# One kernel, two attentions: a query block moved ahead of the first scores, and three output tiles interleaved

## The chip, the cores and the metric

The kernel runs on one core of a Trainium2 chip. A core has TensorE (PE, matrix products), VectorE (DVE), ScalarE (ACT), GpSimd (POOL) and SyncE (SP, which here only issues DMAs). Each engine takes its own instructions in order, and they meet at semaphores. The metric is the device time of one launch in microseconds (us); the smaller, the better.

## The reference

The input is one sequence of 512 tokens of width 1024. Two blocks follow one another:

```
h1 = layer_norm(a*x  + stick_breaking(x) @ mix_wo)          # first attention, over the tokens
h2 = layer_norm(a*h1 + mem_cross_attn(h1, mem) )            # second attention, over 256 memory rows
h3 = layer_norm(a*h2 + (gelu(g) * val) @ ffn_down)          # g, val: h2 @ ffn_up through a short convolution
y  = h3 + rms_norm((gated sum of three branches of rms_norm(h3)) @ w_out)

def mem_cross_attn(h, mem, w_q, w_kv, w_o):                 # 4 heads of 256 columns
    q = heads(h @ w_q);  k, v = heads(split(mem @ w_kv))
    p = softmax(q @ k.T * 256 ** -0.5)
    return merge(p @ v) @ w_o
```

The change is in the second attention, `mem_cross_attn`, and in one helper that three other projections share.

## The kernel before, in words

Activations lie transposed, 128 features on the partitions and 512 tokens along the row, so a tensor of width 1024 is eight tiles of 128x512. float32 products are made out of three faster ones: each operand is cast to a high part (`_hi`, made by ACT) and a remainder (`_lo`, the value minus the high part), and a product is `w_lo*x_hi + w_hi*x_lo + w_hi*x_hi`. One "block" in this text is the three matmuls of one weight block of 128x128 (k counts the eight blocks of a tile), so an output tile is 24 matmuls of 128x512.

**Weights.** They come in units of 128x1024, one unit for one output tile. A ring of four slots holds them. SP loads unit u as soon as PE has counted unit u-4 into `unit_done`; ACT makes `w_hi` in two halves (`split_hi`, line 1551), POOL makes `w_lo` in two halves behind it (line 2261). Each half counts one in `whi_made` or `wlo_made`. ACT and POOL make the units in the order of the program, between their other work. `xq` are the eight query units, `xo` the eight units of the output projection; xo+3 below is the fourth of them. In the stretch of `xo` SP also loads four units of the feed-forward (`extra_stage`, line 535), each right behind a load of the ring (line 533).

**`two_products`** (lines 607 to 636) makes several tiles together in an order of (tile, block) pairs. It issues two matmuls of each block at once and the third, with the remainder of the activation (line 619), four blocks later (`LAG`). It waits for the whole of a unit's `w_lo` before the first block of that tile. **`product`** (lines 584 to 605) makes one tile; it waits for the first half of `w_lo` at block 0, for the second at block 4. `between` and `ahead` put other work into the order.

**Second attention on PE** (lines 863 to 914). Query tiles 0 and 1 are made by `two_products` while the normalization before still delivers `x_hi`, then `xa_scores(0)`. For each of the heads 1 to 3: two query tiles, `xa_turn` of the head before (eight transposes of its probabilities), `xa_scores` of this head (24 matmuls of 128x256 into banks 2 and 3), `xa_values` of the head before (12 matmuls into banks 6 and 7). ACT takes a query tile out of PSUM (line 1556), DVE makes its remainder (line 2684). The softmax of a head goes DVE maximum (2651, 2655), ACT exponential (1690), DVE division (2659). ACT and DVE make `o_hi` and `o_lo` of each half head (1703, 2672).

**Output projection** (lines 936 to 946). `two_products` makes tiles 0 and 1, in the order k = 0..7 with both tiles at each k; before its 11th block it turns head 3, before its 13th it makes head 3's values, whose `o_lo` (counted by `xa_o`) blocks k = 6 and 7 need. Tiles 2 to 5 follow one by one, then tiles 6 and 7 in halves of 256 tokens. A tile's result is taken by DVE: `xo_y` (2710) makes Y = a*H + tile, then `xo_add` and `xo_add_square` add it and its square into running sums; ACT squares it (`xo_square`, 1723).

**ACT's order from head 3 on** matters here:

```
xa_soft(3); split_hi(xo + 2); xa_take(3)
for n in range(7):
    xo_square(n)                 # waits for y of tile n
    if n < 5: split_hi(xo + n + 3)
```

POOL follows with `w_lo` of xo+3 to xo+7 (line 2283), each half when ACT has counted its high part.

Of the kernel before, what the change touches and what calls it, by code (L numbers as in the profile page):

```python
# [6 lines left out]
F32 = mybir.dt.float32  # L7
# [9 lines left out]
KB = D // P  # L17
HD_A = 64
PAIRS = D // P
XA_HEADS = 4  # L20
D_FF = 2816
FFB = D_FF // P
NS = SEQ // P
# [15 lines left out]
U0, _u = {}, 0  # L39
# [6 lines left out]
RING = 4  # L46
# [69 lines left out]
def build_block(nc, w, xT, memT, vec, const, small, pool_count, outT):  # L116
    ctx = ExitStack()
    with ctx:
# [162 lines left out]
        def OUT_BANK(t):  # L281
            return (U0["out"] + (0, 1, 0, 0, 1, 0, 0, 1)[t]) % 2 if t not in (2, 5) else 2
# [25 lines left out]
        JOINT_BANK = [(2, 2, 3, 3, 0, 0), (5, 5, 6, 6, 7, 7)]  # L308
        DOWN_BANK = [4, 1]
        WO_ACC, WO_ACC2 = 7, 5  # L310
        WO_BANKS = [1, 0, 3, 6, 4, 0, 1, 3]
        WO_READ = {5: 2, 6: 1, 7: 3}
        XO_BANK = [{6: 0, 7: 1}, {6: 2, 7: 3}]
# [38 lines left out]
        EV0 = {}  # L352
# [228 lines left out]
        def _(pe):  # L581
            pe.sem_inc(unit_done, CREDIT)

            def product(out, u, slot, hi, lo, ready=None, blocks=8, k0=0, last_k=None, done=True, between=None):


                pe.wait_ge(wlo_made, 2 * u + 1)
                for k in range(blocks):
                    if k == 4:
                        pe.wait_ge(wlo_made, 2 * u + 2)  # L590
                    if between is not None and k in between:
                        between[k]()
                    if ready is not None:
                        pe.wait_ge(*ready(k))
                    if slot is None:
                        wh, wl = unit_hi(u)[:, k * P:(k + 1) * P], unit_lo(u)[:, k * P:(k + 1) * P]
                    else:
                        wh, wl = w_hi[:, slot, k * P:(k + 1) * P], w_lo[:, slot, k * P:(k + 1) * P]
                    first = k0 + k == 0
                    end = k0 + k == (blocks - 1 if last_k is None else last_k)  # L600
                    pe.matmul(out, wl, hi(k), start=first, stop=False)  # L601
                    pe.matmul(out, wh, lo(k), start=False, stop=False)  # L602
                    mm = pe.matmul(out, wh, hi(k), start=False, stop=end)  # L603
                if done:
                    mm.then_inc(unit_done, 1)

            def two_products(u, hi, lo, hi_ready, lo_ready, order=None, ahead=None, banks=None):

                banks = banks or [(u + n) % 2 for n in range(2)]
                order = order or [(n, k) for k in range(4) for n in range(2)] + [(0, 4), (0, 5), (1, 4), (0, 6), (0, 7), (1, 5), (1, 6), (1, 7)]  # L610
                first_n = {n: order.index((n, k)) for n, k in reversed(order)}
                first_k = {k: order.index((n, k)) for n, k in reversed(order)}

                def low(at_n):
                    n, k = order[at_n]
                    b, slot = banks[n], (u + n) % RING
                    if first_k[k] == at_n:
                        pe.wait_ge(*lo_ready(k))
                    mm = pe.matmul(ps[:, b, :], w_hi[:, slot, k * P:(k + 1) * P], lo(k), start=False, stop=(k == KB - 1))
                    if k == KB - 1:  # L620
                        mm.then_inc(unit_done, 1)

                for at_n, (n, k) in enumerate(order):
                    b, slot = banks[n], (u + n) % RING
                    if ahead is not None and at_n in ahead:
                        ahead[at_n]()
                    if first_n[n] == at_n:
                        pe.wait_ge(wlo_made, 2 * (u + n) + 2)
                    if first_k[k] == at_n:
                        pe.wait_ge(*hi_ready(k))  # L630
                    pe.matmul(ps[:, b, :], w_lo[:, slot, k * P:(k + 1) * P], hi(k), start=(k == 0), stop=False)
                    pe.matmul(ps[:, b, :], w_hi[:, slot, k * P:(k + 1) * P], hi(k), start=False, stop=False)
                    if at_n >= LAG:
                        low(at_n - LAG)
                for at_n in range(len(order) - LAG, len(order)):
                    low(at_n)
# [197 lines left out]
            def tile(n, t, hi, lo, between=None):  # L834
                u = U0[n] + t
                if n == "out":
                    if t > 2:
                        pe.wait_ge(evac, t - 2 + (EV0[n] + CREDIT))
                elif n == "wo":
                    if t in WO_READ:  # L840
                        pe.wait_ge(y_made, WO_READ[t] + BEFORE["y_made"]["wo"] + CREDIT)
                elif t != 2:
                    pe.wait_ge(y_made, t + (BEFORE["y_made"][n] + CREDIT - 1))
                bank = OUT_BANK(t) if n == "out" else WO_BANKS[t] if n == "wo" else 6 if t == 2 else u % 2
                product(ps[:, bank, :], u, u % RING, hi, lo, between=between)

            def o_rows(k):
# [54 lines left out]
            for h in range(XA_HEADS):  # L902
                if h == 0:
                    two_products(U0["xq"], x_rows, x_rows_lo, lambda k: (xhi_made, k + 1 + BEFORE["xhi_made"]["wo"]),
                             lambda k: (x_ready, k + 1 + BEFORE["x_ready"]["wo"]))
                for d in range(2 if h else 0):
                    u = U0["xq"] + 2 * h + d
                    pe.wait_ge(evac, EV0["xq"] + 2 * h + d + CREDIT - 1)
                    product(ps[:, u % 2, :], u, u % RING, x_rows, x_rows_lo)
                if h:  # L910
                    xa_turn(h - 1)
                xa_scores(h)
                if h:
                    xa_values(h - 1)
            def xo_sums(half, parts=range(2)):
# [6 lines left out]
            def xo_half(t, half, between):  # L922

                u, o = U0["xo"] + t, ps[:, XO_BANK[half][t], HALF[half]]
                for k in range(KB):
                    if not half and k % 4 == 0:
                        pe.wait_ge(wlo_made, 2 * u + 1 + k // 4)
                    if k in between:
# [6 lines left out]

            pe.wait_ge(evac, EV0["xo"] + CREDIT)
            two_products(U0["xo"], o_rows, o_rows_lo, lambda k: (xa_o, k + 1), lambda k: (xa_o, k + 1),
                         [(n, k) for k in range(KB) for n in range(2)],
                         {10: lambda: xa_turn(XA_HEADS - 1), 12: lambda: xa_values(XA_HEADS - 1)})
            for t in range(2, KB - 2):  # L940
                tile("xo", t, o_rows, o_rows_lo)
            for t in (6, 7):
                pe.wait_ge(y_made, t - 1 + (BEFORE["y_made"]["xo"] + CREDIT))
# [594 lines left out]
        def _(act):  # L1538
# [166 lines left out]
            for h in range(XA_HEADS):  # L1705
                for d in range(2):
                    u = U0["xq"] + 2 * h + d
                    if h:
                        split_hi(u + 2)
                    take(xq_hi[:, 2 * h + d, :], u % 2, u + CREDIT + 1)  # L1710
                if h == 0:
                    split_hi(U0["xq"] + AHEAD)
                if h:
                    xa_take(h - 1)
                xa_soft(h)
            split_hi(U0["xo"] + 2)
            xa_take(XA_HEADS - 1)

            def xo_square(n):
# [766 lines left out]
        def _(dve):  # L2486
# [188 lines left out]
            def xa_parts(h):  # L2675

                two = slice(2 * h, 2 * h + 2)
                if h == 0:
                    dve.wait_ge(evac, EV0["xq"] + CREDIT)
                link(dve.tensor_copy(mk_hi[:, two, :], mem_k[:, two, :]))  # L2680
                dve.tensor_tensor(mk_lo[:, two, :], mem_k[:, two, :], mk_hi[:, two, :].bitcast(F32), ALU.subtract).then_inc(xa_split, 1)
                for d in range(2):
                    dve.wait_ge(evac, EV0["xq"] + CREDIT + 2 * h + d + 1)
                    dve.tensor_tensor(xq_lo[:, 2 * h + d, :], ps[:, d, :], xq_hi[:, 2 * h + d, :].bitcast(F32),
                                      ALU.subtract).then_inc(xa_split, 1)
                two = slice(2 * h * P, (2 * h + 2) * P)
                link(dve.tensor_copy(mv_hi[:, :, two], mem_v[:, :, two]))
                dve.tensor_tensor(mv_lo[:, :, two], mem_v[:, :, two], mv_hi[:, :, two].bitcast(F32), ALU.subtract).then_inc(xa_split, 1)
# [8 lines left out]
            def xo_y(n):  # L2697

                k, half = XO_PARTS[n]
                cols = xo_cols(n)  # L2700
                if half is None:
                    dve.wait_ge(unit_done, U0["xo"] + k + 1 + CREDIT)
                    bank = 6 if k == 2 else k % 2
                else:
                    if half:
                        dve.wait_ge(unit_done, U0["xo"] + k + 1 + CREDIT)
                    else:
                        dve.wait_ge(half_tile_s, k - 5)
                    bank = XO_BANK[half][k]
                dve.scalar_tensor_tensor(out=Y[:, k, cols], in0=H[:, k, cols], scalar=ALPHA, in1=ps[:, bank, cols],  # L2710
                                         op0=ALU.mult, op1=ALU.add).then_inc(y_made, 1)
# [611 lines left out]
```

## Time and profile before

| | |
|---|---|
| median of 3 runs | 1368.56 us (1368.35 to 1369.66) |
| profiled execution | 1367.44 us, its span 1365.7 us |
| PE busy | 1348.8 us, 99% of the span |
| POOL / DVE / ACT busy | 792.0 / 742.4 / 671.5 us |
| granted TensorE clock | full in all 40 slices |

The span is what the profiler sees between the first and the last instruction; 1.74 us of the execution lie outside it. Matmuls are pipelined: a row gives 0.39 us for one of 128x512, but in a stream one starts every 0.227 us. PE's real cost is therefore read from the starts, not from the durations. "Idle before" stands in brackets at the end of a timeline row, with the instruction that ended it.

### The profile page before, as it was taken

The page shows a single profiled execution, that of the slowest core. Times are in us where ns is not written, and L with a number is a line of the kernel's source. Part 1 is how long each engine was busy: PE and PEld are TensorE (multiplying, and loading weights), DVE is VectorE, ACT ScalarE, POOL GpSimd, SP SyncE. Part 2 cuts the span into 40 slices and gives each one's busy share as a digit, 9 for nine tenths or more (in the row PEclk, how much of TensorE's full clock was granted, in tenths as well). Part 3 has the DMA queues.
Part 4 walks back from the last instruction along what each step waited for, and adds up shares of the span by engine and source line. Part 5 has one row for each costly group of instructions (what it writes and reads, how often), then busy time and mean ns, then how long its engine had stood idle before and what let it go on. Part 6 is the DMA issues. An engine that isn't in the chain of part 4 may idle for free.

```text
span 1365.7 us, 24197 instructions
## 1 busy us (share of the span) xinstructions
PE 1348.8 (99%) x9438; PEld 1139.1 (83%) x9438; DVE 742.4 (54%) x995; ACT 671.5 (49%) x1176; POOL 792.0 (58%) x599
## 2 busy tenths in 40 slices
PE   9999999999999999999999999999999999999998
PEld 7888787778899888888888887788888878999987
DVE  5135466465555333333544957344279857777732
ACT  4245665463456444443322578566473435445543
POOL 7653343463466566655665647854268856666782
PEclk9999999999999999999999999999999999999999
DMA  6332221321230232233323212200023222323322
GB/s 228 127 121 77 78 78 47 119 82 62 90 127 32 96 105 92 92 100 100 105 96 109 106 62 93 78 4 4 18 78 124 93 93 93 107 98 106 100 101 77
DMA packets 34508, 122.81 MB, mean 90 GB/s; under 512 B 3824, under 2 KB 4336, under 8 KB 34288
## 3 DMA queue, kind: packets, MB, share of 16 engines
q1 hardware_dynamic: 33696, 119.31, 26.0%
q10 hardware_dynamic: 720, 2.20, 0.5%
q8 instruction: 67, 1.10, 0.3%
q14 instruction: 25, 0.20, 0.0%
HBM read 119.40 MB, written 2.10 MB: 89 GB/s over the span
## 4 chain that ended last, share of the span: by engine, by line
PE 90%; DVE 4%; POOL 2%; ACT 2%; issue 1%; DMA 0%; SPq 0%; ACTq 0%; DVEq 0%; POOLq 0%
PE ps L601 16%; PE ps L602 16%; PE ps L603 16%; PE ps L1452 3%; PE ps L1454 3%; PE ps L1453 3%; PE ps L1521 1%; PE ps L1520 1%; PE ps L1522 1%; PE ps L728 1%; PE ps L753 1%; PE ps L741 1%; PE ps L957 1%; POOL w_lo L2261 1%; PE ps L972 1%; PE ps L973 1%
## 5 line engine op out<-in xcount | busy, mean ns | idle before, releaser
L2261 POOL TENSOR_TENSOR w_lo<-stage,w_hi 128x512 fp32r<-128x512 f32 x378 | 554.1, 1491 | 361.8 <-ACT w_hi L1551 356.9
L1551 ACT ACTIVATE w_hi<-stage 128x512 fp32r<-128x512 f32 x376 | 215.4, 623 | 112.2 <-DMA stage<-w 97.1
L601 PE MATMUL ps<-x_hi,w_lo 128*128 128x512 f32 x664 | 262.6, 395 | 0.0
L602 PE MATMUL ps<-x_lo,w_hi 128*128 128x512 f32 x664 | 258.6, 389 | 0.0
L603 PE MATMUL ps<-x_hi,w_hi 128*128 128x512 f32 x664 | 258.6, 389 | 0.0
L601 PEld LDWEIGHTS ps<-x_hi,w_lo 128*128 128x128 f32 x664 | 124.6, 188 | 29.3 <-issue 2.6
L603 PEld LDWEIGHTS ps<-x_hi,w_hi 128*128 128x128 f32 x664 | 124.6, 188 | 26.3
L602 PEld LDWEIGHTS ps<-x_lo,w_hi 128*128 128x128 f32 x664 | 124.7, 188 | 25.7 <-issue 1.0
L2445 POOL TENSOR_TENSOR w_lo<-stage,w_hi 128x512 fp32r<-128x512 f32 x44 | 75.3, 1743 | 54.0 <-DVE s_val L3165 54.0
L2799 DVE SCALAR_TENSOR_TENSOR conv<-ps,vcol,conv 128x511 f32<-128x511 f32 x44 | 33.0, 749 | 132.2 <-ACT conv L1771 132.0
L1771 ACT ACTIVATE conv<-ps,vcol 128x512 f32<-128x512 f32 x44 | 34.3, 779 | 121.1 <-PE ps L603 120.1
L2549 DVE TENSOR_TENSOR_SCAN ps<-ps,self_one 128x512 f32<-128x512 f32 (+1 forms) x64 | 49.2, 815 | 26.2 <-ACT ps L1613 26.2
L601 PE MATMUL ps<-f_hi,w_lo 128*128 128x512 f32 x154 | 59.9, 389 | 0.0
L602 PE MATMUL ps<-f_lo,w_hi 128*128 128x512 f32 x154 | 59.9, 389 | 0.0
L603 PE MATMUL ps<-f_hi,w_hi 128*128 128x512 f32 x154 | 59.9, 389 | 0.0
L2301 POOL TENSOR_TENSOR f_lo<-conv,f_hi 128x512 f32 (+1 forms) x22 | 28.5, 1297 | 43.6 <-ACT f_hi L1783 43.6
L3174 DVE TENSOR_TENSOR s_lo<-s_val,s_hi 128x512 fp32r<-128x512 f32 x33 | 51.1, 1601 | 0.0
L1383 PE MATMUL ps<-x_hi,w_lo 128*128 128x512 f32 x128 | 50.4, 394 | 0.4 <-POOL w_lo L2261 0.4
L2376 POOL TENSOR_TENSOR Mk<-blk,levels 128x256 f32<-128x256 f32 x40 | 28.5, 731 | 37.5 <-PE ps L1319 16.8
L1385 PE MATMUL ps<-x_hi,w_hi 128*128 128x512 f32 x128 | 49.9, 389 | 0.0
L1384 PE MATMUL ps<-x_lo,w_hi 128*128 128x512 f32 x128 | 49.8, 389 | 0.0
L1520 PE MATMUL ps<-ys_hi,w_lo 128*128 (+1 forms) x96 | 37.5, 390 | 0.0
(516 smaller groups left out, 3316.6 us busy)
## 6 DMA issues: line engine op xcount, KB each, us to landing
stage<-w SPq DMA_DIRECT2D x210, 512.0 KB, 3.3
extra_stage<-w SPq DMA_DIRECT2D x6, 512.0 KB, 5.0
H<-xT SPq DMA_DIRECT2D x3, 512.0 KB, 8.2
mem<-memT SPq DMA_DIRECT2D x2, 512.0 KB, 10.9
pool_n<-pool_count ACTq DMA_DIRECT2D x1, 1024.0 KB, 6.5
outT<-outs SPq DMA_DIRECT2D x4, 256.0 KB, 2.0
outT<-outs SPq DMA_DIRECT2D x2, 384.0 KB, 2.7
stage<-w SPq DMA_DIRECT2D x2, 256.0 KB, 3.5
```

Of the source, the lines that this page charges most:

```text
L601: pe.matmul(out, wl, hi(k), start=first, stop=False)
L602: pe.matmul(out, wh, lo(k), start=False, stop=False)
L603: mm = pe.matmul(out, wh, hi(k), start=False, stop=end)
L1383: pe.matmul(o, wl, x_hi[:, k, :], start=(k == 0), stop=False)
L1384: pe.matmul(o, wh, x_lo[:, k, :], start=False, stop=False)
L1385: mm = pe.matmul(o, wh, x_hi[:, k, :], start=False, stop=(k == KB - 1))
L1520: pe.matmul(o, wl, hi, start=(k == 0), stop=False)
L1551: act.activation(unit_hi(b)[:, cols], unit_stage(b)[:, cols], ACT.Copy).then_inc(whi_made, 1)
L2261: pool.tensor_tensor(unit_lo(b)[:, cols], unit_stage(b)[:, cols], unit_hi(b)[:, cols].bitcast(F32), ALU.subtract).then_inc(wlo_made, 1)
L2445: pool.tensor_tensor(w_lo[:, slot, cols], stage[:, slot, cols], w_hi[:, slot, cols].bitcast(F32), ALU.subtract).then_inc(wlo_made, 1)
L2549: dve.tensor_tensor_scan(z, z, self_one[:, SEQ - n:SEQ][:, ::-1], 0.0, ALU.mult, ALU.add).then_inc(link_s, 1)
L3174: dve.tensor_tensor(s_lo[at_n][:], s_val[at_n][:], s_hi[at_n][:].bitcast(F32), ALU.subtract).then_inc(st_lo_s, 1)
```

## The change

Five edits, all in the second attention but for the first:

1. In `two_products`, a tile's first block waits for the first half of its `w_lo` alone, and block 4 waits for the second half.
2. Query tile 2 goes to bank 6 in place of bank 0 and no longer waits for tile 0's evacuation. Its block k = 0 is issued ahead of `xa_scores(0)`, its other seven behind.
3. `two_products` of the output projection makes tiles 0, 1 and 2 together (banks 0, 1, 2): 24 blocks in place of 16. Ten blocks (k = 0..4 of tiles 0 and 1) come first; then block (2,0), head 3's turn, (0,5), (1,5), head 3's values, (2,1) to (2,5), and k = 6 and 7 of all three tiles. Ahead of (2,0) PE waits for the exponentials of head 3, which read bank 2.
4. The single tiles begin with tile 3.
5. ACT makes `w_hi` of xo+2 before `xa_soft(3)` in place of behind it.

```diff
--- before.py
+++ after.py
@@ -308,6 +308,8 @@
         JOINT_BANK = [(2, 2, 3, 3, 0, 0), (5, 5, 6, 6, 7, 7)]
         DOWN_BANK = [4, 1]
         WO_ACC, WO_ACC2 = 7, 5
+        XQ_BANKS = [0, 1, 6, 1, 0, 1, 0, 1]
+        XO_BANKS = [0, 1, 2, 1, 0, 1]
         WO_BANKS = [1, 0, 3, 6, 4, 0, 1, 3]
         WO_READ = {5: 2, 6: 1, 7: 3}
         XO_BANK = [{6: 0, 7: 1}, {6: 2, 7: 3}]
@@ -625,6 +627,8 @@
                     if ahead is not None and at_n in ahead:
                         ahead[at_n]()
                     if first_n[n] == at_n:
+                        pe.wait_ge(wlo_made, 2 * (u + n) + 1)
+                    if k == KB // 2:
                         pe.wait_ge(wlo_made, 2 * (u + n) + 2)
                     if first_k[k] == at_n:
                         pe.wait_ge(*hi_ready(k))
@@ -839,9 +843,9 @@
                 elif n == "wo":
                     if t in WO_READ:
                         pe.wait_ge(y_made, WO_READ[t] + BEFORE["y_made"]["wo"] + CREDIT)
-                elif t != 2:
+                else:
                     pe.wait_ge(y_made, t + (BEFORE["y_made"][n] + CREDIT - 1))
-                bank = OUT_BANK(t) if n == "out" else WO_BANKS[t] if n == "wo" else 6 if t == 2 else u % 2
+                bank = OUT_BANK(t) if n == "out" else (WO_BANKS if n == "wo" else XO_BANKS)[t]
                 product(ps[:, bank, :], u, u % RING, hi, lo, between=between)
 
             def o_rows(k):
@@ -904,12 +908,14 @@
                     two_products(U0["xq"], x_rows, x_rows_lo, lambda k: (xhi_made, k + 1 + BEFORE["xhi_made"]["wo"]),
                              lambda k: (x_ready, k + 1 + BEFORE["x_ready"]["wo"]))
                 for d in range(2 if h else 0):
-                    u = U0["xq"] + 2 * h + d
-                    pe.wait_ge(evac, EV0["xq"] + 2 * h + d + CREDIT - 1)
-                    product(ps[:, u % 2, :], u, u % RING, x_rows, x_rows_lo)
+                    n, u = 2 * h + d, U0["xq"] + 2 * h + d
+                    if n > 2:
+                        pe.wait_ge(evac, EV0["xq"] + n + CREDIT - 1)
+                    product(ps[:, XQ_BANKS[n], :], u, u % RING, x_rows, x_rows_lo,
+                            between={1: lambda: xa_scores(0)} if n == 2 else None)
                 if h:
                     xa_turn(h - 1)
-                xa_scores(h)
+                    xa_scores(h)
                 if h:
                     xa_values(h - 1)
             def xo_sums(half, parts=range(2)):
@@ -935,9 +941,11 @@
 
             pe.wait_ge(evac, EV0["xo"] + CREDIT)
             two_products(U0["xo"], o_rows, o_rows_lo, lambda k: (xa_o, k + 1), lambda k: (xa_o, k + 1),
-                         [(n, k) for k in range(KB) for n in range(2)],
-                         {10: lambda: xa_turn(XA_HEADS - 1), 12: lambda: xa_values(XA_HEADS - 1)})
-            for t in range(2, KB - 2):
+                         [(n, k) for k in range(5) for n in range(2)] + [(2, 0), (0, 5), (1, 5)] + [(2, k) for k in range(1, 6)]
+                         + [(n, k) for k in range(6, KB) for n in range(3)],
+                         {10: lambda: pe.wait_ge(xa_exp, NS * XA_HEADS), 11: lambda: xa_turn(XA_HEADS - 1),
+                          13: lambda: xa_values(XA_HEADS - 1)}, banks=XO_BANKS)
+            for t in range(3, KB - 2):
                 tile("xo", t, o_rows, o_rows_lo)
             for t in (6, 7):
                 pe.wait_ge(y_made, t - 1 + (BEFORE["y_made"]["xo"] + CREDIT))
@@ -1707,13 +1715,14 @@
                     u = U0["xq"] + 2 * h + d
                     if h:
                         split_hi(u + 2)
-                    take(xq_hi[:, 2 * h + d, :], u % 2, u + CREDIT + 1)
+                    take(xq_hi[:, 2 * h + d, :], XQ_BANKS[2 * h + d], u + CREDIT + 1)
                 if h == 0:
                     split_hi(U0["xq"] + AHEAD)
                 if h:
                     xa_take(h - 1)
+                if h == XA_HEADS - 1:
+                    split_hi(U0["xo"] + 2)
                 xa_soft(h)
-            split_hi(U0["xo"] + 2)
             xa_take(XA_HEADS - 1)
 
             def xo_square(n):
@@ -2681,7 +2690,7 @@
                 dve.tensor_tensor(mk_lo[:, two, :], mem_k[:, two, :], mk_hi[:, two, :].bitcast(F32), ALU.subtract).then_inc(xa_split, 1)
                 for d in range(2):
                     dve.wait_ge(evac, EV0["xq"] + CREDIT + 2 * h + d + 1)
-                    dve.tensor_tensor(xq_lo[:, 2 * h + d, :], ps[:, d, :], xq_hi[:, 2 * h + d, :].bitcast(F32),
+                    dve.tensor_tensor(xq_lo[:, 2 * h + d, :], ps[:, XQ_BANKS[2 * h + d], :], xq_hi[:, 2 * h + d, :].bitcast(F32),
                                       ALU.subtract).then_inc(xa_split, 1)
                 two = slice(2 * h * P, (2 * h + 2) * P)
                 link(dve.tensor_copy(mv_hi[:, :, two], mem_v[:, :, two]))
@@ -2700,7 +2709,7 @@
                 cols = xo_cols(n)
                 if half is None:
                     dve.wait_ge(unit_done, U0["xo"] + k + 1 + CREDIT)
-                    bank = 6 if k == 2 else k % 2
+                    bank = XO_BANKS[k]
                 else:
                     if half:
                         dve.wait_ge(unit_done, U0["xo"] + k + 1 + CREDIT)
```

## Rows read from the trace of the kernel before

**Rows 1.** The page: engines, granted clock by slices, and the chain that ended last.

```profile
PE 1348.8 (99%) x9438; PEld 1139.1 (83%) x9438; DVE 742.4 (54%) x995; ACT 671.5 (49%) x1176; POOL 792.0 (58%) x599
...
PEclk9999999999999999999999999999999999999999
...
PE 90%; DVE 4%; POOL 2%; ACT 2%; issue 1%; DMA 0%; SPq 0%; ACTq 0%; DVEq 0%; POOLq 0%
```

**Rows 2.** Waits of PE, 255 to 400 us: who, for whom, total, times, longest.

```profile
PE ps L873 <- ACT xq_hi L1556: 0.7, 1, 0.7
PE ps L884 <- DVE prob L2659: 0.4, 1, 0.4
```

**Rows 3.** Timeline from 284 us: start, length, engine, line, [idle before].

```profile
285.73 0.50 PE L631 MATMUL ps<-x_hi,w_lo 128*128 128x512 f32 x1 [0.24 <-POOL w_lo L2261]
...
287.21 0.47 PE L631 MATMUL ps<-x_hi,w_lo 128*128 128x512 f32 x1
...
293.40 0.50 PE L631 MATMUL ps<-x_hi,w_lo 128*128 128x512 f32 x1
...
296.03 1.29 PE L619 MATMUL ps<-x_lo,w_hi 128*128 128x512 f32 x5
...
296.68 1.28 ACT L1556 ACTIVATE xq_hi<-ps 128x512 fp32r<-128x512 f32 x2 [1.15 <-PE ps L619]
...
298.01 1.22 PE L873 MATMUL ps<-mk_hi,xq_hi 128*128 128x256 f32 x8 [0.69 <-ACT xq_hi L1556]
```

**Rows 4.** Timeline of POOL, 295 to 296.5 us: first half of unit xq+2.

```profile
295.66 1.48 POOL L2261 TENSOR_TENSOR w_lo<-stage,w_hi 128x512 fp32r<-128x512 f32 x1
```

**Rows 5.** Timeline of PE, 359 to 374.5 us: output projection's first tiles.

```profile
359.09 0.39 PE L619 MATMUL ps<-o_lo,w_hi 128*128 128x512 f32 x1
359.84 1.09 PE L884 MATMUL ps<-con,prob 128*128 128x128 f32 x8 [0.36 <-DVE prob L2659]
...
364.43 0.61 PE L898 MATMUL ps<-pT_lo,mv_hi 128*128 128x512 f32 x2
365.10 0.50 PE L631 MATMUL ps<-o_hi,w_lo 128*128 128x512 f32 x1
365.44 0.40 PE L632 MATMUL ps<-o_hi,w_hi 128*128 128x512 f32 x1
...
367.75 1.30 PE L619 MATMUL ps<-o_lo,w_hi 128*128 128x512 f32 x5
368.88 0.39 PE L601 MATMUL ps<-o_hi,w_lo 128*128 128x512 f32 x1
...
374.32 0.39 PE L601 MATMUL ps<-o_hi,w_lo 128*128 128x512 f32 x1
```

**Rows 6.** Timelines of ACT, DVE and POOL over the same stretch.

```profile
356.38 0.48 ACT L1690 ACTIVATE prob<-ps,soft_max 128x256 f32<-128x256 f32 x1 [2.16 <-DVE soft_max L2655]
...
358.19 1.16 ACT L1551 ACTIVATE w_hi<-stage 128x512 fp32r<-128x512 f32 x2
...
369.57 0.63 ACT L1723 ACTIVATE sqv<-Y 128x512 f32<-128x512 f32 x1 [3.89 <-DVE Y L2710]
370.11 1.14 ACT L1551 ACTIVATE w_hi<-stage 128x512 fp32r<-128x512 f32 x2
...
365.71 0.69 DVE L2672 TENSOR_TENSOR o_lo<-ps,o_hi 128x512 fp32r<-128x512 f32 x1 [0.67 <-ACT o_hi L1703]
368.85 0.69 DVE L2710 SCALAR_TENSOR_TENSOR Y<-H,ps 128x512 f32<-128x512 f32 x1 [2.45 <-PE ps L619]
...
370.84 0.68 DVE L2710 SCALAR_TENSOR_TENSOR Y<-H,ps 128x512 f32<-128x512 f32 x1
...
370.80 5.06 POOL L2261 TENSOR_TENSOR w_lo<-stage,w_hi 128x512 fp32r<-128x512 f32 x4 [8.62 <-ACT w_hi L1551]
```

**Rows 7.** From issue to landing, lines 533 (ring) and 535 (extra units).

```profile
L533 SPq DMA_DIRECT2D stage<-w x4: 328/333/432, 368.8 to 380.0; - x4
...
DMA to landing us min/median/max: 3.6/4.1/6.0
...
DMA to landing us min/median/max: 4.5/5.0/7.9
```

## The prediction

> **What bounds the kernel now.** The page comes first. PE is busy 99% of the span, the chain that ended last lies on it for 90%, and its clock is granted in full throughout [rows 1]. So time is gained only where PE stands still, and any standing of PE that the change adds is paid in full. Second, PE's waits in the stretch of the second attention: little is left to win, 0.7 us ahead of the first scores and 0.4 us ahead of head 3's turn [rows 2]. The profile counts a wait only after the matmul before it has drained, so the starts in the timeline give the true holes, and they are what I sum. The scale is the stream: five matmuls start between 367.75 and 368.88 us, 0.227 us each [rows 5], so a block of three is 0.68 us and a tile of 24 is 5.44 us, which is also what lies between the starts of tiles 2 and 3, 368.88 and 374.32. Last, the timelines of ACT, DVE and POOL over the same stretch say what each hole waits for [rows 6].
>
> I found no other hole of PE up to 440 us: behind tile 3 of the output projection its stream has none. A shift of tile 3 is therefore carried to the end, unless something below re-forms.
>
> **Halves of the remainders (edit 1).** At query tile 1 PE waits 0.24 us for POOL's second half (285.73). With half the wait it starts up to that much earlier, but the third activation block is taken when `x_hi` arrives (287.21), and the last one, at 293.40, also on arrival [rows 3]. ACT makes these at its own pace, so what is won is lost at the next arrival. Value 0; bounds 0 and a gain of 0.24. The waits added at block 4 of each tile are one more instruction each, with POOL ahead by then. In the first attention's projection and in the last one PE shows no wait for `w_lo` inside `two_products`. Value 0.
>
> **One query block ahead of the scores (edit 2).** The last five matmuls of query tiles 0 and 1 start from 296.03, so PE is free at 296.03 + 5 x 0.227 = 297.17. ACT needs until 297.96 for the two query tiles, and the scores start at 298.01 [rows 3]. The hole is 0.84 us. The block put there needs the first half of `w_lo` of xq+2: POOL has it at 295.66 + 1.48 = 297.14 [rows 4], practically when PE is free. The block takes 0.68 us, to 297.9, and still fits in front of 298.01. It is taken out of tile 2 behind the scores, where PE streams. **Gain 0.68 us.** Bounds: nothing, if POOL is late by more than the hole, and 0.84. The bank is free and nothing else is queued behind it but the scores themselves.
>
> **Three tiles together (edits 3 and 5): what it fills.** Before head 3's turn PE is free at 359.09 + 0.23 = 359.32 and starts at 359.84: 0.52 us, for the division of the softmax. Behind head 3's values it is free at 364.43 + 2 x 0.227 = 364.88 and starts at 365.10, and the matmul behind that one starts 0.34 us later where 0.227 is the rule: 0.22 + 0.11 = 0.33 us [rows 5]. After the change block (2,0) stands in the first hole: 0.68 us against 0.52, so the turn itself moves back by 0.16 but PE never stands. In the second stand five blocks of tile 2, 3.4 us of work. The last `o_lo` came at 365.71 + 0.69 = 366.40 [rows 6], 1.5 us behind the values' end, so it comes in time too. **Gain 0.52 + 0.33 = 0.85 us.**
>
> What it needs: `w_lo` of xo+2 at 359.3. Before, ACT made its `w_hi` from 358.19, so POOL's first half came too late for that. Edit 5 puts it into the 2.16 us in which ACT idles before the exponentials at 356.38 [rows 6]; it takes 1.16 us and is covered by them. From 354.22 it ends at 355.4; POOL, idle then, is half a piece behind and at 1.48 us a half [rows 4] ends both by about 358. Cost 0. The added wait for the exponentials: ACT is through with the four of them and on to `w_hi` at 358.19 [rows 6], one microsecond ahead. Cost 0; queued behind it is everything on PE, so if they were late the loss would be one for one.
>
> **What it uncovers.** Before, tile 2 alone (5.44 us) ran on PE between the end of tiles 0 and 1 and the start of tile 3. Under it ran a chain that nobody else waited for: the last matmul of tile 0, the fourth of the five, starts at 367.75 + 3 x 0.227 = 368.43; DVE starts y of tile 0 at 368.85; ACT squares it at 369.57; only then, in ACT's order, comes `split_hi` of xo+3 at 370.11; POOL starts at 370.80 and needs 5.06 / 4 = 1.27 us for a half [rows 5, 6]. That is 372.07, 3.64 us behind the last matmul of tile 0, and tile 3 started at 374.32: covered with 2.25 us to spare.
>
> After the change tiles 0, 1 and 2 end within three matmuls. The last of tile 0 is the third from the end, so PE is free 3 x 0.227 = 0.68 us behind its start, and next in its order is tile 3. The chain is unchanged: xo+3 still stands behind the square of tile 0, and the diff moves xo+2 only. **PE stands 3.64 - 0.68 = 2.96 us**, and 0.11 for the slow second start behind a wait: 3.07 us. The other wait of tile 3, for y of tile 1, ends sooner: y1 started 370.84 - 368.85 = 1.99 us behind y0 and takes 0.68, against 3.22 us from y0's start to POOL's half [rows 6]. The second half comes 1.27 us later; four blocks take 2.7. Bounds of this term: 2.7 (a release as quick as can be) and 3.6 (DVE or ACT a step later).
>
> **Behind it.** Tile 4's unit is loaded when tile 0 is counted. At the shortest landing of 3.6 us [rows 7], then 0.7 for ACT's first half and 1.27 for POOL's, its `w_lo` is there about 6.0 us behind tile 0's last matmul; PE wants it at 3.76 + 5.44 = 9.2. Later tiles have more room.
>
> **The sum**, against the profiled execution: 1367.44 - 0.68 - 0.85 + 3.07 = 1368.98, that is +1.54 us. The profiled execution is 1.12 us below the median of the runs, so the same step on the median gives 1368.56 + 1.54 = **1370.1 us**, 0.11% more. A difference of under 0.2%, 2.7 us, can hardly be told from none here; my forecast is within it, on the slow side.
>
> **Rivals.**
>
> *The clock falls in the new hole (slower).* PE stands about 3 us in a place where it now never does; the granted clock is 2.4 GHz in every slice, and the longest wait in those rows is 0.7 us [rows 1, 2], so nothing here shows what 3 us do. If the clock fell to 1.2 GHz, a matmul of the stream would start every 0.45 us, 0.227 more. It decides from (2.7 - 1.54) / 0.227, six matmuls at the lower level, on: half of tile 3 would add 2.7, all of it 5.4, so 1372.8 to 1375.5. Against it: the hole is short and dense work lies on both sides. The Trainium skill, "TensorE: Matmul & The Clock Gate", Part 1, says that a PE left idle goes back to 1.2 GHz and must be busy again before it gets 2.4 GHz; by that rule the hole would be paid twice, and no run here shows it. Chance 0.12.
>
> *The fourth tile doesn't wait (the gain stays).* It would take a `w_hi` of xo+3 made earlier, or a quicker chain. Its load is in the ring already (at 370.11 ACT went from the square straight to it, with no idle between [rows 6]), so only ACT's order is in the way; I read that order as binding. Then -0.68 - 0.85 = -1.53, 1367.0 us: also within 0.2%. For faster by more, both bounds and the scatter would have to add. Chance 0.08.
>
> *The loads crowd.* Three ring slots come free at once, so six loads of 512 KB queue where four did. If tile 4's took 7.9 us, the longest here [rows 7], its `w_lo` would come at 10.3 against 9.2: 1.1 us more, 1371.2. But it is issued first. Chance 0.06.
>
> *The query block costs instead of filling*, POOL's half being late: by 0.3 us its gain is gone, with the rest as forecast: 1370.8. Chance 0.07.
>
> **Chances and range.** The forecast as summed has 0.67. Nearly all of the clock's 0.12 is slower; of the crowding and of the forecast's own scatter (the runs of before span 1.3 us) I give 0.06 more. Faster has 0.03, same 0.79, slower 0.18. The likeliest case is 1369.4 to 1371.0; the range reaches down towards the uncovered case and up to the edge of the clock's: 1367.8 to 1372.8.
>
> **What the profile after would show.** Right: block (2,0) of the queries between 297.2 and 297.9 and scores at about 298.0; no idle ahead of the turn and behind the values; PE waiting for `w_lo` (line 2261) at the first matmul of tile 3, about 3 us, the only large wait in the stretch, and its chain y, square, `w_hi`, `w_lo` with nothing between; matmuls 0.227 us apart behind it. Wrong: no such wait, or a spacing of 0.45 us behind it, or a second wait at tile 4 for a DMA, or an idle ahead of the query block longer than what it fills.

## The result and the profile after

The changed kernel takes 1372.88 us (median of 8 runs, 1371.06 to 1374.85) against 1368.45 us for the kernel before (8 runs beside it, 1368.08 to 1369.66). The ratio is 1.0032, with a 95% interval of 1.0023 to 1.0041: slower, by 4.4 us. The forecast was 1370.1 with a range up to 1372.8, and 0.79 on "same"; the time lies just above the range. Launches of 1906 us and more (two of the kernel before and three of the experiments) are left out here and below.

The page of the kernel after, to be read against [rows 1]. PE has the same 9438 instructions and is busy 4.7 us longer. At the grain of 40 slices the clock still looks full.

```profile
PE 1353.5 (99%) x9438; PEld 1141.5 (83%) x9438; DVE 745.9 (54%) x995; ACT 670.7 (49%) x1176; POOL 793.4 (58%) x599
...
PEclk9999999999999999999999999999999999999999
```

PE's waits, 255 to 420 us, the counterpart of [rows 2]: the wait of the scores for `xq_hi` is gone, the one for the probabilities is not, and a new one for `w_lo` stands on top.

```profile
PE ps L603 <- POOL w_lo L2270: 3.0, 1, 3.0
PE ps L635 <- ACT x_hi L1682: 0.8, 1, 0.8
PE ps L888 <- DVE prob L2668: 0.5, 1, 0.5
```

PE's timeline in the two places of the change. The columns are those of [rows 3].

```profile
298.05 1.30 PE L621 MATMUL ps<-x_lo,w_hi 128*128 128x512 f32 x5
299.18 0.48 PE L603 MATMUL ps<-x_hi,w_lo 128*128 128x512 f32 x1
...
300.03 1.22 PE L877 MATMUL ps<-mk_hi,xq_hi 128*128 128x256 f32 x8
...
361.32 0.40 PE L621 MATMUL ps<-o_lo,w_hi 128*128 128x512 f32 x1
362.23 1.09 PE L888 MATMUL ps<-con,prob 128*128 128x128 f32 x8 [0.51 <-DVE prob L2668]
...
374.52 1.29 PE L621 MATMUL ps<-o_lo,w_hi 128*128 128x512 f32 x5
378.77 0.47 PE L603 MATMUL ps<-o_hi,w_lo 128*128 128x512 f32 x1 [2.95 <-POOL w_lo L2270]
379.07 0.51 PE L604 MATMUL ps<-o_lo,w_hi 128*128 128x512 f32 x1
379.38 0.63 PE L605 MATMUL ps<-o_hi,w_hi 128*128 128x512 f32 x1
379.81 0.63 PE L603 MATMUL ps<-o_hi,w_lo 128*128 128x512 f32 x1
...
382.37 0.51 PE L603 MATMUL ps<-o_hi,w_lo 128*128 128x512 f32 x1
382.72 0.39 PE L604 MATMUL ps<-o_lo,w_hi 128*128 128x512 f32 x1
...
385.94 0.39 PE L603 MATMUL ps<-o_hi,w_lo 128*128 128x512 f32 x1
```

Three things are to be seen. The query block stands in the hole ahead of the scores. Ahead of the turn there is still a hole (361.32 to 362.23, where the stream would take 0.23). And behind the wait for `w_lo` the matmuls start 0.43 us apart from 379.38 to 382.37, then 0.227 again: tile 3, from 378.77 to 385.94, takes 7.17 us instead of 5.44. The windows show why (start and end, length, then busy time and instructions of PE, PEld, DVE, ACT and POOL, granted clock, DMA share, GB/s): the granted clock, 1.00 up to 378 us, is 0.50 from 380 to 382, so it fell from 2.4 to 1.2 GHz behind a stand of PE of 3 us.

```profile
376.00:378.00 2.00, 0.00 (x0) 0.00 (x0) 1.97 (x4) 1.67 (x3) 0.65 (x1) 1.00 0.75 233
378.00:380.00 2.00, 1.23 (x4) 1.01 (x5) 1.97 (x4) 1.58 (x3) 2.00 (x3) 0.80 1.04 373
380.00:382.00 2.00, 2.00 (x7) 1.52 (x6) 1.42 (x3) 0.72 (x2) 2.00 (x2) 0.50 0.95 363
382.00:386.00 4.00, 4.00 (x18) 3.28 (x17) 0.00 (x0) 1.15 (x2) 2.88 (x3) 0.92 0.75 301
```

The chain that the hole waits for, in the timeline of DVE, ACT and POOL, is the one of [rows 6], and nothing stands between its links:

```profile
375.40 0.69 DVE L2719 SCALAR_TENSOR_TENSOR Y<-H,ps 128x512 f32<-128x512 f32 x1 [6.61 <-PE ps L621]
...
376.12 0.63 ACT L1732 ACTIVATE sqv<-Y 128x512 f32<-128x512 f32 x1 [8.06 <-DVE Y L2719]
...
376.66 1.13 ACT L1559 ACTIVATE w_hi<-stage 128x512 fp32r<-128x512 f32 x2
...
377.35 5.00 POOL L2270 TENSOR_TENSOR w_lo<-stage,w_hi 128x512 fp32r<-128x512 f32 x4 [18.64 <-ACT w_hi L1559]
```

**Where the time went.** I compare the start of the same matmul in the two profiled executions (after minus before) at marks that both have. It is +2.02 us just ahead of the changed stretch (297 us), +1.35 behind the query block (317), +1.34 behind the three tiles (374), and +6.18 behind tile 3 (380). So the query block gives -0.67, the three tiles 0.0, the hole 3.11 (378.77 less the 375.66 at which the stream would go on) and tile 3 itself 7.17 - 5.44 = 1.73. Of this 0.12 is the slow start behind a wait (in `g9` below tile 3 takes 5.56 us behind a wait at full clock) and **1.61 the low clock**. The stretch gives -0.67 + 0.0 + 3.11 + 0.12 + 1.61 = **+4.17 us**, and the medians differ by 4.43.

Of the +2.02 at 297 us, 1.94 arise in the first 15 us, in code that the diff doesn't touch. Much of it is a slow pace at the start, which lasts longer in this execution. In the timelines of PE, after and then before, the same four matmuls take 9.86 - 8.15 = 1.71 us, 0.43 each, and 7.46 - 6.49 = 0.97 us, from start to start (the granted clock reads 1.00 there in both, so the pace is read from the starts):

```profile
8.15 1.91 PE L669 MATMUL ps<-w_hi,x_lo 128*128 128x512 f32 x4
9.86 1.43 PE L672 MATMUL ps<-w_lo,x_hi 128*128 128x512 f32 x4
...
6.49 1.14 PE L665 MATMUL ps<-w_hi,x_lo 128*128 128x512 f32 x4
7.46 1.07 PE L668 MATMUL ps<-w_lo,x_hi 128*128 128x512 f32 x4
```

This shift from 297 to 380 us is what I call **the stretch** below. The rest scatters from one profiled execution to the next: 0 to 2.0 us ahead of the stretch, up to 3.2 us from 780 us on, where PE in some profiles stands for "issue".

### The profile page after: what moved, and what is told of

Its sections match the earlier page's. It is cut to its first block, busy times and chain, and to the rows that moved or that the text cites. A ratio compares the mean times of both kernels' runs of the same rounds, so it can differ in the third digit from the quotient of the medians.

```text
span 1373.1 us, 24201 instructions
## 1 busy us (share of the span) xinstructions
PE 1353.5 (99%) x9438; PEld 1141.5 (83%) x9438; DVE 745.9 (54%) x995; ACT 670.7 (49%) x1176; POOL 793.4 (58%) x599
## 4 chain that ended last, share of the span: by engine, by line
PE 93%; DVE 3%; ACT 2%; issue 1%; POOL 1%; DMA 0%; SPq 0%; ACTq 0%; POOLq 0%; DVEq 0%
PE ps L603 16%; PE ps L604 16%; PE ps L605 16%; PE ps L1460 3%; PE ps L1462 3%; PE ps L1461 3%; PE ps L1391 2%; PE ps L1393 2%; PE ps L1392 2%; PE ps L1529 1%; PE ps L1528 1%; PE ps L1530 1%; PE ps L732 1%; PE ps L757 1%; PE ps L745 1%; PE ps L685 1%
```

## The experiments

Ratios are to runs of the kernel before on the same chip, with 95% intervals. The intervals are 1.2 to 1.6 us either way, so small terms are read from the stretch, in one profiled execution of each kernel. "Whole run" is (ratio - 1) x 1368.5 us; for the changed kernel it is +4.4. Of each launch the mean granted clock is recorded as well, to three places: 3 us at half the clock are 0.001 of a launch.

### 1. What the fourth tile waits for

`e1_fourth_unit_early`: the changed kernel, with the fourth unit split ahead of the squares.

```diff
             xa_take(XA_HEADS - 1)
+            split_hi(U0["xo"] + AHEAD)
...
-                if n < 5:
+                if 0 < n < 5:
                     split_hi(U0["xo"] + n + AHEAD)
```

> The changed kernel, with one more unit pulled forward in ScalarE's order: the high part of xo+3 is made straight behind head 3's values in place of behind the square of tile 0. Theory A (the 4.4 us are one hole ahead of tile 3, 3.1 us, and the lower clock behind it, 1.7 us): both vanish, no matmul spacing of 0.43 us is left in the output projection, and the time is 0.3 to 1.0 us under the kernel before, 1367.4 to 1368.2. Rival B (the lower clock or the loss has another cause, the three-tile order itself or the crowded loads): the time stays at least 1.5 us above the kernel before.

Measured: 1371.27 us, ratio 1.0018 (1.0009 to 1.0027). A miss by 3 us. The wait for `w_lo` is gone and another stands in its place, in the timeline:

```profile
375.52 1.29 PE L621 MATMUL ps<-o_lo,w_hi 128*128 128x512 f32 x5
...
378.39 0.68 DVE L2720 SCALAR_TENSOR_TENSOR Y<-H,ps 128x512 f32<-128x512 f32 x1
...
379.12 0.69 PE L603 MATMUL ps<-o_hi,w_lo 128*128 128x512 f32 x1 [2.31 <-DVE Y L2720]
379.61 0.63 PE L604 MATMUL ps<-o_lo,w_hi 128*128 128x512 f32 x1
```

Tile 3 goes to bank 1, which y of tile 1 must read first. That wait ends 2.46 us behind the place where the stream would go on (376.66), 0.65 us less than the hole before. The clock fell here too. To take away the longest wait of several is worth only the distance to the next. `f9_unit_and_bank` takes both away; against e1 it has this more:

```diff
-        XO_BANKS = [0, 1, 2, 1, 0, 1]
+        XO_BANKS = [0, 1, 2, 3, 0, 1]
...
-                else:
+                elif t > 3:
                     pe.wait_ge(y_made, t + (BEFORE["y_made"][n] + CREDIT - 1))
```

> The kernel of e1 (unit xo+3 early), and tile 3 goes to bank 3, which is free, in place of bank 1, so it no longer waits for DVE's y of tile 1, the wait of 2.3 us that took the place of the 3.0 us one. Theory A: no hole ahead of tile 3, no matmul spacing of 0.43 us behind it; tile 4's remainder, 6.0 us behind tile 0's last matmul by the trace of e1, comes just as PE asks for it, 6.1 us behind. Total: the query block's 0.7 us stay, about 1367.8, 3 us and more under e1. Rival B: the hole only moves on to tile 4 (its load, issued when tile 0 ends, comes later): a wait for its w_lo of 1 us or more there, total 1369 or more.

Measured: 1368.11 us, ratio 0.9991 (0.9982 to 1.0). The hole is gone and so is the low clock; from 359 to 380 us the shift grows by 0.16 us, where it grew by 4.8 in the changed kernel and by 4.2 in e1. The whole runs of e1 and f9 are +2.5 and -1.2 us, 3.7 apart; their stretches from 359 us on differ by 4.05, which without the clock's 1.6 would be 2.4.

From 297 us on the stretch is +4.9 in e1 and +0.8 in f9, 2.4 and 2.0 more than their whole runs. In both profiles the shift grows by 0.65 us from 297 to 317 us, where it falls by 0.67 in the changed kernel: PE waits 1.3 to 1.4 us for `mk_lo` there (last section). Whether it was so in their other launches isn't recorded.

### 2. The query block and the halves alone

`e3_query_block_only` is the kernel before with edit 2; `f4_halves_only` the kernel before with edit 1. Their diffs are the parts of the diff shown above.

> The kernel before with the query block alone ahead of the first scores (bank 6 for query tile 2, no other edit). Theory A, from the two traces: 0.66 us less than before, 1367.8, scores starting one block later in PE's order but at the same time. Rival: the block delays the scores, since the remainder of xq+2 is ready only as PE is: 0 or a small loss.

> The kernel before with edit 1 alone, the halves of the remainders awaited. As predicted: 0 (within 0.3 us), query tile 1 starting up to 0.3 us earlier at its first block and nothing left of it at the arrival of the third activation block. Rival: the further waits in PE's queue cost some tenths.

Measured: e3 1368.48 us, ratio 0.9998 (0.9989 to 1.0007); f4 1368.72 us, ratio 0.9997 (0.9987 to 1.0006). Neither can be told from none by the whole run, and the 1367.8 expected of e3 was not reached. By the stretch e3 gains 0.67 us, f4 nothing (+0.06).

### 3. Why the three tiles gained nothing

`e8_split_moved_only` is the kernel before with edit 5: `split_hi(U0["xo"] + 2)` ahead of `xa_soft(3)`.

> The kernel before with the high part of xo+2 made ahead of head 3's softmax in place of behind it, nothing else. Theory A (GpSimd's subtraction of 128x512, now under the softmax chain, holds up VectorE's small scaling of the maximum, 1.21 us in the changed kernel where it took 0.17): that scaling takes about 1.2 us, PE's hole ahead of head 3's turn grows from 0.52 to about 1.5 us, total 1.0 us above the kernel before, 1369.5. Rival: a coincidence of that one profile; scaling 0.17 us, total unchanged.

Measured: 1370.08 us, ratio 1.001 (1.0001 to 1.0019), the stretch +1.05. The timeline of POOL, DVE and PE:

```profile
355.02 2.54 POOL L2262 TENSOR_TENSOR w_lo<-stage,w_hi 128x512 fp32r<-128x512 f32 x2 [6.97 <-ACT w_hi L1551]
...
356.38 1.21 DVE L2656 TENSOR_SCALAR soft_max<-soft_max 128x4 f32<-128x4 f32 x1
...
361.07 1.09 PE L884 MATMUL ps<-con,prob 128*128 128x128 f32 x8 [1.39 <-DVE prob L2660]
```

DVE's scaling of 128x4 maxima lasts 1.21 us and ends at 357.59, within 0.03 us of the end of POOL's two subtractions (355.02 + 2.54 = 357.56). The exponentials, the division and the turn wait behind it. The same instruction in the timeline of DVE before, with POOL idle beside it, and in the changed kernel:

```profile
356.18 0.17 DVE L2655 TENSOR_SCALAR soft_max<-soft_max 128x4 f32<-128x4 f32 x1
...
357.53 1.21 DVE L2664 TENSOR_SCALAR soft_max<-soft_max 128x4 f32<-128x4 f32 x1
```

`f10_all_three` is f9 with the split of xo+2 moved further up, between ACT's takes of head 2, where POOL's work meets nothing that a turn waits for (the line at its old place goes):

```diff
                     act.activation(pT_hi[:, h % 2, m, :], ps[:, 4 + m, :], ACT.Copy).then_inc(xa_pT, 1)
+                if h == XA_HEADS - 2:
+                    split_hi(U0["xo"] + 2)
```

> The kernel of f9, and ScalarE makes the high part of xo+2 one step earlier, between head 2's two transposed probabilities and its outputs, so that GpSimd's subtraction is over before VectorE scales head 3's maximum. Theory A: that scaling takes 0.17 us again, the 0.7 us hole ahead of head 3's turn closes, total 0.8 us under f9, about 1367.0, 1.5 us under the kernel before. Rival: the earlier subtraction holds up another VectorE instruction (the cast or the subtraction of the values of the memory) and nothing is won against f9.

Measured: **1367.70 us**, ratio 0.999 (0.9981 to 0.9998), the fastest version here, if by little: 1.0 us under the kernel before by the medians, 1.4 by the ratio. The stretch is -1.47 (+1.34 to -0.13). From the timelines of DVE, then of PE: the scaling takes 0.17 us, the turn follows the stream at once, and tile 3 follows the three tiles at once.

```profile
356.85 0.17 DVE L2665 TENSOR_SCALAR soft_max<-soft_max 128x4 f32<-128x4 f32 x1
...
360.44 0.39 PE L621 MATMUL ps<-o_lo,w_hi 128*128 128x512 f32 x1
360.67 1.03 PE L888 MATMUL ps<-con,prob 128*128 128x128 f32 x8
...
372.91 1.30 PE L621 MATMUL ps<-o_lo,w_hi 128*128 128x512 f32 x5
374.04 0.39 PE L603 MATMUL ps<-o_hi,w_lo 128*128 128x512 f32 x1
```

### 4. The clock alone: the hole kept, but filled

The changed kernel, with N matmuls more ahead of tile 3, so that PE stands for less time in the same hole:

```diff
+            for n in range(12):
+                pe.matmul(ps[:, 3, :], o_hi[:, 0, 0:P], o_hi[:, 1, :], start=True, stop=True)
             for t in range(3, KB - 2):
```

`e5` has N = 12 (`g5` is a repeat of it), `f6` N = 5, `g9` N = 9.

> The changed kernel with 12 extra matmuls of 128x512 into the free bank 3 ahead of tile 3, extra work that nobody reads: 12 x 0.227 = 2.7 us of work in the 3.1 us hole. Tile 3 still starts when its remainder is ready. Theory A (PE's standing still is what takes the clock down): clock full behind it, tile 3 in 5.44 us, total 1.6 to 1.9 us under the changed kernel, about 1371.1. Rival B (the clock falls for another reason, or the hole's length isn't what counts): no less than the changed kernel, 1372.9.

> The changed kernel with 5 extra matmuls ahead of tile 3 (work that nobody reads), so that PE stands for about 2.0 us in place of 3.1. Theory A with the clock falling even for shorter standing (e1 fell after 2.3 us): seven or eight matmuls 0.43 us apart behind the hole, stretch as long as in the changed kernel. Rival: 2.0 us are too short and the clock stays full, tile 3 takes 5.44 us, the stretch is 1.7 us shorter.

> The changed kernel with nine matmuls of 128x512 ahead of tile 3, whose output (bank 3) nobody reads. They run for 9 x 0.227 = 2.04 us of the hole, so between the starts of the last of them and of tile 3 lie about 3.34 - 2.04 = 1.3 us, and PE waits some 0.9. If the length of the stand decides, the clock stays at the upper level, since stands of 1.8 us between starts passed without a fall: the stretch from 297 to 380 us is then +2.4 us against before and tile 3 takes 5.4 us. If any wait for w_lo there brings the fall (the same code that fell with five fillers), the stretch is +4.2 and the matmuls of tile 3 start 0.43 us apart for a while.

> The hole filled with twelve matmuls, once more. The stretch from 297 to 380 us is +2.4 to +2.6 us against before, without a low clock, as it was. If the first whole-run median (1373.17) was scatter of the later stages, this one lies near 1368.45 + 2.5 = 1371; if the twelve bring a loss of their own behind the stretch, it lies near 1373 again, and the trace shows about 2 us more behind 780 us.

| kernel | wait for `w_lo` | clock behind it | stretch | whole run | launches with mean clock under 1.000 |
|---|---|---|---|---|---|
| after, N = 0 | 2.95 | 1.2 GHz, 7 intervals of 0.43 | +4.16 | +4.4 | 7 of 8 |
| f6, N = 5 | 1.82 | 1.2 GHz, 7 intervals of 0.43 | +4.18 | +3.7 | 3 of 6 |
| g9, N = 9 | 0.93 | 2.4 GHz | +2.56 | +3.4 | 0 of 8 |
| g5, N = 12 | 0.26 | 2.4 GHz | +2.58 | +3.3 | 1 of 8 |
| e5, N = 12 | 0.26 | 2.4 GHz | +2.60 | +4.1 | 2 of 10 |

For the stretch all four expectations held. Tile 3 starts in the same place against the rest whatever is in the hole, so the stretch differs by the clock alone: 1.6 us. It fell behind a wait of 1.82 us:

```profile
373.62 1.29 PE L949 MATMUL ps<-o_hi 128*128 128x512 f32 x5
376.73 0.47 PE L603 MATMUL ps<-o_hi,w_lo 128*128 128x512 f32 x1 [1.82 <-POOL w_lo L2272]
...
377.53 0.63 PE L603 MATMUL ps<-o_hi,w_lo 128*128 128x512 f32 x1
377.96 0.63 PE L604 MATMUL ps<-o_lo,w_hi 128*128 128x512 f32 x1
```

and not behind one of 0.93 us in the same place:

```profile
375.38 2.20 PE L949 MATMUL ps<-o_hi 128*128 128x512 f32 x9
378.50 0.47 PE L603 MATMUL ps<-o_hi,w_lo 128*128 128x512 f32 x1 [0.93 <-POOL w_lo L2272]
378.81 0.39 PE L604 MATMUL ps<-o_lo,w_hi 128*128 128x512 f32 x1
379.04 0.40 PE L605 MATMUL ps<-o_hi,w_hi 128*128 128x512 f32 x1
...
384.06 0.39 PE L603 MATMUL ps<-o_hi,w_lo 128*128 128x512 f32 x1
```

The expectation for N = 12 of the whole run missed: it should have been 1.7 us below the changed kernel, and the three without the low clock have +3.6 on average, where the two with it have +4.0. So the whole runs don't confirm the clock's 1.6 us. The last column gives one part of the answer: the clock seems not to fall in every launch. Among launches of one kernel those whose mean clock is under 1.000 are the longer ones: in f6 the three of them have a median of 1374.83 us and the other three 1371.83; in e1 seven have 1371.82 and four 1370.6; in the changed kernel seven have 1372.94 and the one at 1.000 is its fastest, 1371.06. That is 1.2 to 3.0 us between launches of one program, which fits the 1.6 of the profile, from few launches. (The mean doesn't say where in the launch the clock was low. At the end of a launch it falls as well, in the profile of e3 to 0.50 from 1366 us to the end of the span at 1366.9, and 7 of 34 launches of before have a mean under 1.000 too.)

For the other part, a control asks whether the extra matmuls themselves cost something later: `g12_three_plus_12` is f10 with the same twelve.

> The best version so far (fourth unit early, third unit early, own bank) with twelve matmuls of 128x512 more ahead of tile 3, whose output (bank 3) tile 3 overwrites unread. PE streams through that place, so the twelve cost 12 x 0.227 = 2.72 us and nothing else if extra matmuls cost only their own time: that version's ratio of 0.999 (1.04 us below before) plus 2.72, about 1370.3 us, ratio 1.0013. The rival, that twelve more instructions on PE disturb something later in the program (which would explain why the hole filled with twelve did not lower the whole run's median although its stretch was 1.7 us shorter): 1372 or more, with the difference behind 780 us in the trace.

Measured: 1371.28 us against 1369.16 for the kernel before, ratio 1.0016 (1.0007 to 1.0024), whole run +2.2: 1.1 us more than its stretch of +1.11, and g9, g5 and e5 have 0.8, 0.7 and 1.5 more than theirs. In its profile the shift goes from +1.54 at 795 us to +2.65 at 800 and +4.69 at 985, PE standing 0.9 and 0.8 us for "issue". The 1371.28 us lie between the two answers (1370.3, or 1372 and more). e5, g5 and g9 show the same step of +1.1 between 795 and 800, as do after and e3, with no filler. So about a microsecond of the filled kernels' whole runs comes from far behind the stretch and not from the hole; what causes it stays open.

## Why the prediction was wrong

**The hole: right.** Predicted from the starts 2.96 us, and 3.07 with the slow second start, from the chain y, square, `w_hi`, `w_lo`; measured 3.11, and 3.23 with it. (The 2.95 of the timeline is the wait as the profile counts it, from where the matmul before has drained.) e1 and f9 show that this chain and the bank behind it are all of it.

**The query block: right.** -0.68 predicted, -0.67 in the changed kernel and in e3 alone. **The halves: right**, 0 in f4.

**The clock: the first step that failed.** "If the clock fell to 1.2 GHz" was a rival with 0.12, priced at 2.7 to 5.4 us, "against it: the hole is short and dense work lies on both sides". It is what happened, in the profile and, as far as the mean clock tells, in most launches, but it cost less: seven intervals of 0.43 us and slower ones at both ends, 1.61 us in all, not half a tile (2.7) or a whole one (5.4). That the measured 1372.88 lies beside this rival's 1372.8 is luck: there the clock alone makes up the difference to the forecast, here it is the clock's 1.6 and the step that comes next. The sum left this term at nothing. No row of before had a stand of this length on PE, so none could speak for the hole being short enough; 0.12 had no row behind it. The Trainium skill, "TensorE: Matmul & The Clock Gate", Part 1, says that an idle PE falls back to 1.2 GHz and is given 2.4 GHz again only once it has been busy. The trace agrees in kind, with the 0.50 granted from 380 to 382 us.

**Edit 5 "Cost 0": the second step that failed.** "POOL, idle then" was right, but I asked only what POOL needed, not what ran beside it. POOL's subtractions now lie over DVE's scaling of the maxima of head 3, and DVE's small instruction takes 1.21 us where it took 0.17: 1.04 us at the head of the chain on which the turn waits (e8: +1.05). That eats the 0.85 us of the filled holes; in the changed kernel the two cancel to 0.0, and f10, without it, has -0.80 there (-1.47 + 0.67). The Trainium skill, "SBUF — State Buffer", section "SBUF: two separate sides", says that GpSimd and those VectorE instructions that work in a two-port mode or have two inputs in SBUF share a port pair as an exclusive lock, which whichever starts first keeps for its whole instruction. That the scaling works in such a mode no view shows, but its times agree: in e8 the scaling began 0.09 us behind the start of POOL's second subtraction (355.02 + 1.27 = 356.29, against 356.38) and ended with it.

**The other wait of tile 3.** "For y of tile 1, ends sooner" was true, by 0.65 us. So the statement changed nothing for the sum, but the rival "the fourth tile doesn't wait", with 1367.0 us for an early `w_hi`, was wrong: e1 is that case, and it has 1371.27.

**The sum again.** Predicted -0.68 - 0.85 + 3.07 = +1.54. Measured -0.67 + 0.0 + 3.23 + 1.61 = +4.17. The miss of 2.6 us is the clock's 1.6, the 0.85 that edit 5 took back, and 0.16 by which the hole was longer.

**What is shown and what is open.** Each term of the sum is shown by an experiment in the stretch, of one profiled execution a kernel. In whole runs the changed kernel and f10 are 4.4 + 1.4 = 5.8 us apart by the ratios (5.5 by the medians), where their stretches differ by 5.63; without the clock's part it would be 4.0. Open is what holds the filled kernels about a microsecond above their stretches, and with it the clock's share in a median: between 1.2 and 3.0 us by launches of one kernel, 0.4 by the filled ones, with intervals wider than that. I did not try the changed kernel with only the bank changed, or with only the split of xo+2 moved further up.

## What to carry to other kernels

Before tiles are interleaved so that they end together, list everything that starts when the first of them ends (here the square, the next unit's split, a bank's release) and ask what PE does meanwhile: here a tile of 5.44 us had covered two waits, of 3.1 and 2.5 us, and taking the longer away alone left the shorter. A new stand of PE of 2 or 3 us behind dense work is to be priced at its length plus the slow matmuls that may stand behind it (here 1.6 us). Work moved into an idle stretch of GpSimd is to be laid beside VectorE's timeline too, above all beside small instructions at the head of a chain.

## What the runs showed of the hardware

- The clock, by the granted clock and the spacing of the 128x512 matmuls: it fell from 2.4 to 1.2 GHz behind waits of PE of 2.95 (after), 2.31 (e1) and 1.82 us (f6), each behind a dense stream, and was back after seven intervals of 0.43 us in all three. In other launches of the same kernels the mean clock is 1.000, so no such fall can lie in them. In the profiles it did not fall behind waits of 1.39 (e8), 0.93 and 0.26 us. It fell not at the wait but a little behind it: in f6 PE had started three matmuls at 0.31, 0.23 and 0.26 us before the first at 0.43.
- VectorE held up beside GpSimd: 128x4 scaling 1.21 us in place of 0.17. The same befell the cast of `mem_k` in e1 and f9 (timeline of POOL and DVE in f9): 3.98 us in place of the 1.46 of before and after. It ended 0.29 us behind the last of the three instructions of POOL below (296.12 + 2.52 = 298.64), and PE stood 1.4 us for the `mk_lo` behind it. In the profile of before the same cast began 0.1 us behind the start of a POOL instruction too and got through behind that one; what decides between the two isn't shown.

```profile
294.86 1.29 POOL L2287 TENSOR_TENSOR x_lo<-H,x_hi  x1
294.95 3.98 DVE L2690 CAST mk_hi<-mem_k 128x512 fp32r<-128x512 f32 x1 [3.27 <-ACT mem_k L1598]
...
296.12 2.52 POOL L2271 TENSOR_TENSOR w_lo<-stage,w_hi 128x512 fp32r<-128x512 f32 x2
```
